# Start-up loads, one load behind a norm, and the last tile of a streaming encoder layer on eight cores

## The reference

```python
h = _rmsnorm(x, norm1_g)
z = h @ w_in                                    # 1024 -> 1536 = [a | u | v]
a = z[..., :512]; u = gelu(z[..., 512:1024]); v = gelu(z[..., 1024:])
pool_out, new_hist = _pool_mixer(a, pool_hist, pos0, pool_w, pool_scale)
gmlp_out = _gmlp_gate(u, v, gmlp_ws, gmlp_b)
x = x + concatenate([pool_out, gmlp_out], axis=-1) @ w_out
f = _rmsnorm(x, norm2_g) @ w_up                 # 1024 -> 4096
x = x + square(relu(f)) @ w_down                # 4096 -> 1024
y = _rmsnorm(x, normf_g)                        # after the layer
```

## Time and profile before

| | |
|---|---|
| median of 3 runs | 1279.29 us (1278.93 to 1279.64) |
| profiled execution | 1281.59 us |
| its span on the slowest core (core 1) | 1280.0 us |
| spans of the eight cores | 1272.7 to 1280.0 us |
| PE busy, core 1 | 1247.8 us, 97% |
| DVE, ACT, POOL busy | 516.1, 374.2, 102.0 us |
| DMA | 238.78 MB, mean 187 GB/s |

### The profile page before, as it was taken

The page is one execution under the profiler, slowest core; times in us unless marked ns, Lnnn a source line. Parts: engine busy times, 40 slices in busy tenths (PEclk is TensorE's granted clock), DMA queues, the critical chain, the costliest instruction groups (busy, mean ns, idle before and its releaser), DMA issues.

```text
span 1280.0 us, 19211 instructions; the slowest of 8 cores (1272.7 to 1280.0 us)
## 1 busy us (share of the span) xinstructions
PE 1247.8 (97%) x6815; PEld 657.2 (51%) x6815; DVE 516.1 (40%) x946; ACT 374.2 (29%) x719; POOL 102.0 (8%) x183
## 2 busy tenths in 40 slices
PE   8999999999799999999999999999999999999996
PEld 3555545556444554554455456445545545554552
DVE  5664434442433443443344354234525433440312
ACT  4453313134312431332133033223404322320410
POOL 4110000011001100100000010000001000000000
PEclk9999999999799999999999999999999999999998
DMA  8998958439435737943953794386378448437751
GB/s 176 164 232 188 225 146 168 133 107 313 140 132 172 229 143 196 282 162 133 238 207 132 225 283 145 139 239 219 133 221 255 165 144 247 155 138 233 255 198 49
DMA packets 87503, 238.78 MB, mean 187 GB/s; under 512 B 54497, under 2 KB 54689, under 8 KB 64625
## 3 DMA queue, kind: packets, MB, share of 16 engines
q1 hardware_dynamic: 74482, 185.09, 45.9%
q0 software_dynamic: 12928, 52.47, 18.1%
HBM read 213.62 MB, written 34.43 MB: 194 GB/s over the span
## 4 chain that ended last, share of the span: by engine, by line
PE 94%; DMA 2%; DVE 1%; issue 1%; SPq 1%; ACT 0%; POOL 0%; DVEq 0%; POOLq 0%; ACTq 0%
PE ps L724 29%; PE ps L693 27%; PE ps L415 9%; PE ps L577 9%; PE ps L675 7%; PE ps L655 6%; PE ps L440 4%; DMA yall<-X 2%; PE ps L335 1%; PE ps L368 1%; SPq L345 1%; PE ps L378 1%; PE ps L515 1%; PE ps L534 0%; DMA ST<-rows 0%
## 5 line engine op out<-in xcount | busy, mean ns | idle before, releaser
L693 PE MATMUL ps<-H2T,RING 128*128 128x384 bf16 x2304 | 387.4, 326 | 0.0
L724 PE MATMUL ps<-RING,ST 128*128 128x512 bf16 x1728 | 374.9, 379 | 0.0
L693 PEld LDWEIGHTS ps<-H2T,RING 128*128 128x128 bf16 x2304 | 224.3, 98 | 147.9
L724 PEld LDWEIGHTS ps<-RING,ST 128*128 128x128 bf16 x1728 | 169.1, 98 | 202.4
L300 ACT ACTIVATE JUNK<-X 128x1024 bf16<-128x1024 f32 (+1 forms) x103 | 106.2, 1031 | 442.6 <-DVE X L729 316.7
L697 ACT ACTIVATE ST<-ps 128x384 bf16<-128x384 f32 x288 | 140.2, 489 | 212.1 <-PE ps L693 212.0
L699 DVE TENSOR_TENSOR ST<-ST 128x384 bf16<-128x384 bf16 x288 | 95.8, 355 | 175.5 <-ACT ST L697 175.1
L729 DVE TENSOR_TENSOR X<-ps,X 128x512 f32<-128x512 f32 x54 | 37.1, 691 | 232.5 <-PE ps L724 232.5
L415 PE MATMUL ps<-HT,WAU 128*128 128x384 bf16 (+1 forms) x640 | 109.5, 332 | 3.2 <-ACT HT L339 2.5
L577 PE MATMUL ps<-WOUT,MIXT 128*128 128x512 bf16 x480 | 105.2, 379 | 1.3 <-DVE MIXT L553 0.9
L415 PEld LDWEIGHTS ps<-HT,WAU 128*128 128x128 bf16 x640 | 63.1, 99 | 48.9 <-issue 9.3
(11 more groups left out here) (96 smaller groups left out, 691.6 us busy)
## 6 DMA issues: line engine op xcount, KB each, us to landing
RING<-scr SPq DMA_DIRECT2D x144, 1024.0 KB, 5.9
RING<-w_mlp POOLq DMA_DIRECT2D x16, 1024.0 KB, 14.6
scr<-RING SPq DMA_DIRECT2D x16, 1024.0 KB, 10.6
yall<-X POOLq DMA_DIRECT2D x30, 512.0 KB, 11.4
X<-xall POOLq DMA_DIRECT2D x27, 512.0 KB, 5.8
X<-xall SPq DMA_DIRECT2D x6, 512.0 KB, 8.2
WOUT<-w_out POOLq DMA_DIRECT2D x2, 1024.0 KB, 20.0
WAU<-w_au POOLq DMA_DIRECT2D x3, 512.0 KB, 7.1
```

Source lines behind the costliest of these rows:

```text
L693: i_ = e.matmul(bank(ub)[:, 0:TOK], lhsT=RING[s][:, k, (m % 4) * 128:(m % 4 + 1) * 128], rhs=H2T[:, k, :], start=(k == 0), stop=(k == 7))
L724: i_ = e.matmul(bank(n)[:, :], lhsT=ST[:, kg * 8 + kk, n * 128:(n + 1) * 128], rhs=RING[s][:, kk, :], start=(kg == 0 and kk == 0), stop=(k ...
```

## The change

It has five parts.

1. Start. `rows` and the halo are loaded from ACT's queue as its first two instructions; SP issues all six x tiles of both first supertiles, without waiting in between. The halo's square, root and scaling come first or early on ACT, POOL and DVE. All five row broadcasts stand before line 415, with fewer warm matmuls between them (5, then 3, 3, 2 and 2 instead of 5 and three times 8), all in PSUM bank 3. The `WAU` loads wait for later x tiles than before. The transposes of supertile 1 stand between the groups of line 415.
2. Pair stage. The first two UP groups of supertile 1 come before the first DN of supertile 0.
3. Supertile 2. `gen_L(4)` comes after norm 1 of supertile 3 on POOL, and the last two UP groups before `gen_WI_au(3)` come after the transposes of that norm.
4. Supertile 2, DN. The eight mixer pieces of supertile 3 are dealt out one or two at a time between DN groups, and the output projection of supertile 3 moves behind the fourth round.
5. End. `gen_tile_final` is replaced by `gen_tail` and `gen_tail_out`. The last tile's last half is worked in two parts of 256 columns in all four rounds; the gain is multiplied in before the root is known; the scaling by the root is split between ACT and DVE; ACT and SP issue the stores of their own halves.

```diff
+        add("act", lambda e: e.dma_start(out=ROWS[:, 0:2 * D + 512], in_=rows[:, :]), writes=ROWk, dma="su1")
+        add("act", lambda e: e.dma_start(out=XH, in_=xh[:, :]), writes=[("X", 2, 0)], dma="su2")
         add("act", lambda e: e.activation(out=JUNK[:, 0:4], in_=WSMTS[:, 0, 0:4], func=AF.Gelu_apprx_tanh),
...
-        load_x(0, n1=1)
-        add("sp", lambda e: e.dma_start(out=ROWS[:, 0:2 * D + 512], in_=rows[:, :]), writes=ROWk, dma="su1")
-        load_x(0, n0=1)
-        add("sp", lambda e: e.dma_start(out=XH, in_=xh[:, :]), writes=[("X", 2, 0)], dma="su2")
+        load_x(0)
+        load_x(1)
...
-        load_x(1, [("X", 0, 2)])
...
+        def gen_tail(i, n, hh, c0, c1, ub, col, last_part):
+            b = i % NXB
+            t = i * NT + n
+            XG = X[(i + 2) % NXB]
+            add("dve", lambda e: e.tensor_tensor(out=X[b][:, n, c0:c1], in0=bank(ub)[:, 0:c1 - c0],
+                                                 in1=X[b][:, n, c0:c1], op=ALU.add),
+                writes=[("X", b, n), ("BANK", ub)])
+            norm_square("f2"[hh], col, X[b][:, n, c0:c1], [("X", b, n)])
+            add("dve", lambda e: e.tensor_tensor(out=XG[:, n, c0:c1], in0=X[b][:, n, c0:c1], in1=GFB[:, c0:c1], op=ALU.mult),
+                reads=["GFB", ("X", b, n)], writes=[("X", (i + 2) % NXB, n), ("XG", n, hh)])
+            S = SS["f2"[hh]][:, col:col + 1]
...
+            if not last_part:
+                add("dve", lambda e: e.tensor_tensor(out=SSE[:, n:n + 1], in0=S, in1=SSE[:, n:n + 1], op=ALU.add),
+                    reads=[("SSc", "2", col)], writes=[("SSE", n)])
+                return
+            add("pool", lambda e: e.tensor_tensor(out=RS["f"][:, n:n + 1], in0=S, in1=SSE[:, n:n + 1], op=ALU.add),
+                reads=[("SSc", "2", col), ("SSE", n)], writes=[("RS", "f", n)])
+            norm_pow("f", n, n + 1)
+
+        def gen_tail_out(i, n):
...
+            add("act", lambda e: e.activation(out=XG[:, n, 0:512], in_=XG[:, n, 0:512], func=AF.Copy, scale=R),
+                reads=[("RS", "f", n)], writes=[("XG", n, 0)])
+            add("dve", lambda e: e.tensor_scalar(out=XG[:, n, 512:1024], in0=XG[:, n, 512:1024], scalar1=R, scalar2=None,
+                                                 op0=ALU.mult),
+                reads=[("RS", "f", n)], writes=[("XG", n, 1)])
+            for hi, q in enumerate(("act", "sp")):
+                fin_y[(n, hi)] = add(q, lambda e, hi=hi: e.dma_start(
+                    out=yall[t * 128:(t + 1) * 128, hi * 512:hi * 512 + 512], in_=XG[:, n, hi * 512:hi * 512 + 512]),
+                    reads=[("XG", n, hi)], dma=f"yend_{n}_{hi}")
...
+                split = i == NS - 1 and hh == 1 and n == NT - 1
+                for part in range(2 if split else 1):
+                    p0, p1 = (256 * part, 256 * part + 256) if split else (0, 512)
...
         gen_pair_UP(0, 6, 8, (0,))
+        gen_pair_UP(0, 0, 2, (1,))
         gen_pair_DN(0, 0, 0)
         gen_N1_elem(2)
-        gen_pair_UP(0, 0, 8, (1,))
+        gen_pair_UP(0, 2, 8, (1,))
...
-            gen_L(3 + h)
+            if h == 0:
+                gen_L(3)
...
                 gen_N1_elem(3)
-                gen_UP(i, 18, 28)
+                gen_L(4)
+                gen_UP(i, 18, 26)
                 gen_N1_T(3)
+                gen_UP(i, 26, 28)
                 gen_WI_au(3)
...
-                gen_DN(i, 0, 2)
-                gen_WO_pe(3)
+                gen_DN(i, 0, 0, mid=[[], [], pieces[0:1]])
+                gen_DN(i, 0, 1, mid=[pieces[1:2], pieces[2:3], pieces[3:5]])
+                gen_DN(i, 0, 2, mid=[pieces[5:6], pieces[6:7], pieces[7:8]])
...
             gen_DN(i, 0, 3, tile_final=last)
             if i == 2:
+                gen_WO_pe(3)
                 gen_N2_elem(3)
```

140 lines of the change are left out of this document (63 added, 77 removed).

## The result

The changed kernel takes 1266.18 us (median of four executions, 1266.04 to 1266.38) against 1279.29: a ratio of 0.9898, 95% interval 0.9878 to 0.9917. It is faster by 13.1 us; 20.3 were forecast, and 1266.2 lies above the range of 1255 to 1264.5.

The account below looks back on a forecast made before the run. TensorE was taken to bound the kernel, with gains only at start, passage and tail. Gains 12.8 + 5.8 + 1.4 + 1.0 + 0.2 = 21.2 from the profiled 1281.59 gave 1260.4; median forecast 1259.0, range 1255 to 1264.5 us.

Parts of the forecast that it names:

- A: Passage into supertile 2: x load behind norm 3 and 16 UP matmuls behind its transposes remove PE's pause; gain 12.8 us.
- C: Pair stage: two UP groups ahead of the first DN cover PE's wait for ACT and DVE; gain 1.4 us.
- D: Supertile 2's DN: dealing supertile 3's pieces between DN groups removes two PE waits on DVE; gain 1.0 us.
- Rival 3: Passage: PE still waits, because of supertile 3's x load or DVE; gain there 2 instead of 12.8, 1270 us; chance 0.04.
- 2.3 us between profile and median: Whole run: profiled time above median before; if the distance stays 1258.1 us, if it was a shorter passage pause 1260.4.
- B: Start: fewer warm matmuls, rows loaded sooner, and no H2T wait let PE gain 5.8 us.
- 14 warm matmuls, 14 x 0.216 = 3.0 us: Start: dropping 14 warm matmuls takes their time at the high clock level, 3.0 us, off PE's path.
- I let the level rise when it rose before: Start: PE's clock assumed to go high between 13.3 and 17.2 us as before, so earlier rows count half, 0.95 us.
- Rival 4: Start: fewer warm matmuls leave PE's clock low past line 415 or longer; 1269 to 1282 us; chance 0.03.
- two more rounds of DN, 10.4 us, stand between: Supertile 2's DN: later output projection still leaves 10.4 us before norm 2's transposes, against 7.1 needed at the passage.
- rival 1: Start becomes bound by loads, with WAU pieces late; the start's gain falls to about 1, 1264 us; chance 0.13.
- rival 2: Start: the halo lands late, delaying HB and WAU; the start's gain falls to about 2.5, 1262.5 us; chance 0.10.

Follow-up runs that it names:

- p_only: Kernel before the change, with only the x load of supertile 4 queued behind norm 3 on POOL; 1272.1 to 1273.7 us, ratio 0.9928.
- p_both: Kernel before the change, with that x load moved and 16 UP matmuls put behind the transposes of norm 3; 1268.3 to 1273.1 us, ratio 0.9899.
- s_best: Changed kernel with three later row broadcasts back between projection groups and 8 warm matmuls ahead of each of three transposes; 1262.6 to 1270.7 us, ratio 0.9875.
- s_warm: Changed kernel with 8 warm matmuls instead of 3, 3 and 2 ahead of the first three transposes, row broadcasts still between; 1264.0 to 1273.3 us, ratio 0.9895.
- t_pe: Changed kernel with the transposes of norm 2 of supertile 3 made by TensorE instead of DMA; 1265.1 to 1266.1 us, ratio 0.9870.
- t_gate: Changed kernel with DMA transposes for supertile 3's norm 2 and supertile 4's norm 1 issued some 3 us behind a ring load; 1263.2 to 1264.1 us, ratio 0.9855.
- t_early: Changed kernel with the DMA transposes of norm 2 of supertile 3 issued one DN round earlier; 1273.0 to 1274.4 us, ratio 0.9937.
- best: s_best with supertile 3's norm 2 transposes on TensorE and supertile 4's norm 1 transposes one DN round earlier; 1263.3 to 1270.7 us, ratio 0.9866.
- best_gate: Changed kernel with the start of s_best and the later-issued DMA transposes of t_gate; 1262.1 to 1269.4 us, ratio 0.9852.
- best_tail: best with the stores of ACT's halves of the first two final tiles issued by POOL; 1265.1 to 1267.6 us, ratio 0.9874.

## Why the prediction was wrong

**Right.** What bounded the passage, and its size: A 13.1 for 12.8, with both halves needed, as the working had it (p_only, p_both). C and D within 0.4. Steady stages unchanged. Rival 3 fell. The 2.3 us between profile and median went with the pause and did not stay; 1259.0 had split the difference.

**Wrong: B, 1.85 instead of 5.8.** The step that failed is "14 warm matmuls, 14 x 0.216 = 3.0 us", beside "I let the level rise when it rose before". The two exclude each other: with them, eight in a row, the level rose by 16 us on every core, and with ten in pieces between row broadcasts the low level lasted to 26 us on core 1. Core 1 did not pay for the 14 matmuls, but paid at half clock for what came after: some 2.9 us in three broadcasts, 1.2 in the transposes, 1.3 in line 414. On cores with the high level by 13 us (s_best, four of s_warm), which all have the warm matmuls in, the v projection begins at 45.3 to 46.7, 2.1 to 3.5 ahead of the mean of before, 48.75: about the 5.8 less the 3.0 that were never free. Rival 4 was the right mechanism, but its price was asked only for the case that the low level outlasts line 414; the mild case, a few us, was the likely one and had no chance of its own.

**Wrong: the transposes of norm 2 were not priced.** In D, "two more rounds of DN, 10.4 us, stand between" covers the norm's elementwise work, and HB was indeed there at 378.27 + 3.67 = 381.9. But SP issues the three DMA transposes only behind the ring load that follows the first of those rounds, at 385.17, and UP wants them at 394.98. In the trace of before they landed 8.9 after their first issue (402.60 to 411.50, core 1), which would have left 0.9; they took 11.5. In its place the runs showed a wait of 1.6 to 2.2 on one core of each pair. It cost 3.85 on core 1, the half clock behind it included, and about 2 on the other three. With the transposes on PE (t_pe), or issued later (t_gate), it is gone, which shows that the transposes were the wait. That they were late by the ring load ahead of them is read from the landings; why a second core's ring load is slower stays open.

**The other rivals.** No PE wait for WAU (rival 1). The halo was late (rival 2): its square, first on ACT, waited to 7.52, and the first WAU piece was issued at 11.04; PE's slow row work hid that. By the Trainium skill, "DMA: Bandwidth & Descriptors", section "Issuing engines are not separate DMA queues", a second queue saves only the time of the issue. The trace differs: one issue is 0.4 (1.07 for 1.51), and the rows began 1.3 earlier, so a queue of their own brought more here.

**Open.** Why single cores are 7 to 8 us late in one execution of several kernels. In two that were profiled (7.1 on core 2 of s_warm, 5.1 on core 6 of p_both) it was the third transpose of HT, issued just ahead of POOL's stores of y (at 404.32 and 404.50 on the first), as in t_early. In s_best, best and best_gate the long core has no profile, but its mean granted clock is 0.991, 0.991 and 0.990 against 0.997 to 0.998 on the others. Taken as time at half clock that is (0.997 - 0.991) x 1269 / 0.5 = 15 us, of which half is lost: an estimate of 7.6 us, about what these cores are longer. So there it is likely the clock; where it fell is not known, and core 6 of best_tail shows one such place in the start. Open too is how a neighbour's ring load comes to stand ahead.

## What to carry to other kernels

Warm matmuls are not idle filler that can be counted at their busy time: ask first what the clock does without them, keep them in one unbroken run, and put row broadcasts behind them. A DMA that something waits for has to be priced from its issue to its landing, with whatever moves at that moment: a large load right ahead of it in the same queue, stores of another queue, a load of instructions. Where neighbouring cores run in step their loads may count too; here that is argued, not tried by itself. When a pause is removed, ask what it had kept apart.
